# First stage of a two-block transformer kernel: positions loaded later, and the first chunk's second half fetched, rounded and split ahead of the second tokens' x

## The reference

```python
def rms_norm(x, g):
    xf = x.astype(jnp.float32)
    y = xf * lax.rsqrt(jnp.mean(xf * xf, axis=-1, keepdims=True) + NORM_EPS)
    return (y * g.astype(jnp.float32)).astype(x.dtype)

def moba_attention(xn, w_qkv, w_o, cos, sin):
    qkv = (xn @ w_qkv).reshape(b, s, 3, N_HEADS, HEAD_DIM)
    q, k, v = [jnp.transpose(qkv[:, :, i], (0, 2, 1, 3)) for i in range(3)]
    q = apply_partial_rope(q, cos, sin)
    k = apply_partial_rope(k, cos, sin)
    ...

def first_block(x, positions, norm_mix, ...):
    cos, sin = rope_tables(positions)
    for i in range(DEPTH):
        xn = rms_norm(x, norm_mix[i])
        ...
```

## Time and profile before

| what | value |
|---|---|
| device time, three runs | 1088.93, 1090.29 and 1090.34 us, median 1090.29 |
| profiled execution: first to last instruction (span) | 1086.7 us |
| PE busy | 1073.5 us, 99% of the span, 5810 matmuls |
| DVE busy | 740.5 us, 68% |
| ACT busy | 560.8 us, 52% |
| POOL busy | 40.2 us, 4% |
| data moved | 195.83 MB, 180 GB/s over the span |

### The profile page before, as it was taken

How to read it: one execution, slowest core, us unless ns; L and a number is a source line. 1 busy time by engine, 2 the same in 40 slices (tenths; PEclk the granted TensorE clock), 3 DMA queues, 4 the chain that set the end, 5 groups by cost and what they waited for, 6 DMA issues and landing times.

```text
span 1086.7 us, 15287 instructions
## 1 busy us (share of the span) xinstructions
PE 1073.5 (99%) x5810; PEld 908.4 (84%) x5810; DVE 740.5 (68%) x1044; ACT 560.8 (52%) x723; POOL 40.2 (4%) x59
## 2 busy tenths in 40 slices
PE   8999999999999999999999999999999999999997
PEld 6888888888888888888878888888889778888886
DVE  5756665656686656568877975665897878666665
ACT  5556444435455444346665544445653766444453
POOL 1000000000000000000000220000300300000000
PEclk9999999999999999999999999999999999999999
DMA  9953366564547564637532755657576324754651
GB/s 332 338 168 116 92 218 212 155 217 169 171 148 236 179 207 158 228 106 204 176 110 78 237 191 195 193 165 255 156 237 228 92 79 156 232 185 163 206 180 39
DMA packets 127162, 195.83 MB, mean 180 GB/s; under 512 B 6977, under 2 KB 97217, under 8 KB 126994
## 3 DMA queue, kind: packets, MB, share of 16 engines
q1 hardware_dynamic: 123904, 185.77, 51.8%
q0 software_dynamic: 3216, 9.51, 3.0%
q10 hardware_dynamic: 2, 0.00, 0.0%
HBM read 194.21 MB, written 1.05 MB: 180 GB/s over the span
## 4 chain that ended last, share of the span: by engine, by line
PE 95%; DVE 3%; ACT 1%; issue 1%; DVEq 0%; DMA 0%; ACTq 0%
PE ps L2099 25%; PE ps L2000 15%; PE ps L2002 15%; PE ps L2001 15%; PE ps L2102 13%; PE ps L2181 2%; PE ps L2220 1%; PE ps L2042 1%; PE ps L2597 1%; PE ps L2183 1%; DVE act L1237 1%; PE ps L2246 1%; PE ps L2595 1%; PE ps L2632 1%; PE ps L2279 1%
## 5 line engine op out<-in xcount | busy, mean ns | idle before, releaser
L2099 PE MATMUL ps<-act,whi 128*128 128x512 f32 x1200 | 424.4, 397 | 0.0
L1112 DVE TENSOR_TENSOR wlo<-raw,whi 128x2048 fp32r<-128x2048 f32 (+2 forms) x161 | 363.9, 2277 | 87.5 <-ACT whi L672 87.1
L2102 PE MATMUL ps<-act,wlo 128*128 128x256 f32 x1200 | 336.7, 281 | 0.0
L672 ACT ACTIVATE whi<-raw 128x2048 fp32r<-128x2048 f32 (+2 forms) x170 | 317.6, 1887 | 26.7 <-PE ps L2002 20.6
L2099 PEld LDWEIGHTS ps<-act,whi 128*128 128x128 f32 x1200 | 225.2, 188 | 53.7
L2102 PEld LDWEIGHTS ps<-act,wlo 128*128 128x128 f32 x1200 | 226.7, 189 | 2.0
L2002 PE MATMUL ps<-whi,hlo 128*128 128x512 f32 x400 | 157.1, 393 | 0.0
L2000 PE MATMUL ps<-whi,hhi 128*128 128x512 f32 x400 | 156.7, 392 | 0.1
L2001 PE MATMUL ps<-wlo,hhi 128*128 128x512 f32 x400 | 156.6, 392 | 0.0
L2000 PE MATMUL ps<-whi,act 128*128 128x512 f32 (+2 forms) x286 | 112.4, 393 | 1.5 <-DVE act L1812 0.6
L2002 PE MATMUL ps<-whi,act 128*128 128x512 f32 (+2 forms) x286 | 108.0, 378 | 0.0
(11 more groups left out here) (230 smaller groups left out, 1154.5 us busy)
## 6 DMA issues: line engine op xcount, KB each, us to landing
raw<-mlp_w_up_in SPq DMA_DIRECT2D x32, 1024.0 KB, 6.5
raw<-mlp_w_down_in SPq DMA_DIRECT2D x32, 1024.0 KB, 4.9
raw<-ffn_w_gate_in SPq DMA_DIRECT2D x22, 1024.0 KB, 5.4
raw<-ffn_w_up_in SPq DMA_DIRECT2D x22, 1024.0 KB, 5.3
raw<-ffn_w_down_in SPq DMA_DIRECT2D x22, 1024.0 KB, 4.9
raw<-attn_w_qkv_in SPq DMA_DIRECT2D x10, 1024.0 KB, 9.2
raw<-w_kv_shared_in SPq DMA_DIRECT2D x8, 1024.0 KB, 5.3
raw<-attn_w_o_in SPq DMA_DIRECT2D x4, 1024.0 KB, 5.0
```

The costliest lines, as they stand in the source:

```text
L672: nc.scalar.activation(whi[:, s, 0:width], raw[:, s, 0:width], ACT.Copy).then_inc(hi_ready, 1)
L1112: nc.vector.tensor_tensor(wlo[:, s, 0:width], raw[:, s, 0:width], whi[:, s, 0:width].bitcast(F32), ALU.subtract).then_inc(lo_ready, 1)
L2099: nc.tensor.matmul(bank(b + f), lhsT=w[0][:, at:at + P], rhs=act[:, k, :, :].rearrange("p a t -> p (a t)"), start=k == 0, stop=False, skip ...
L2102: ins = nc.tensor.matmul(bank(b + f, 0, T), lhsT=w[1][:, at:at + P], rhs=act_hi[:, k, :], start=False, stop=k == KT - 1, skip_group_check= ...
```

## The change

SP loads half b of chunk 0 ahead of the second tile's x. POOL issues the positions behind its wait for `hi_ready`. ACT rounds half b right after half a, ahead of its copies of quarters 1 and 2. DVE makes both low parts of chunk 0 right after the split of quarter 0, and then, for the second tile, x of quarter 2, split of 2, x of 3 and split of 1. PE signals each half of the spread gain row by itself; it runs two fillers ahead of quarter 0, six behind quarter 1 and none ahead of quarter 2; and it goes through chunks 0 and 1 tile by tile (all four row blocks of a chunk for one tile, then for the other), with quarter 2 transposed behind the first tile's products of chunk 0 and quarter 3 behind the second tile's first six.

```diff
@@ SP @@
             sp.dma_start(x[:, 0, :], x_rows[:, 0, :]).then_inc(x_loaded, 16)
             load_half(0, 0, first_half_loaded)
+            load_half(0, 1, w_loaded[SLOT[0]])
             sp.dma_start(x[:, 1, :], x_rows[:, 1, :]).then_inc(x_rest_loaded, 16)
-            load_half(0, 1, w_loaded[SLOT[0]])
             load_half(1, 0, second_half_loaded)
@@ POOL @@
+            pool.wait_ge(hi_ready, 2)
             for n, name in enumerate(("positions", "positions_2")):
                 pool.dma_start(pos_i[:, n, :], a[name].rearrange("a (t p) -> p (a t)", p=P),
                                allow_slow_non_contiguous=True).then_inc(pos_loaded, 16)
-            pool.wait_ge(hi_ready, 2)
@@ ACT @@
             copy_turned("mix0", (0,))
             hi_part_of(0, 0, first_half_loaded, first_half_hi)
-            copy_turned("mix0", (1, 2))
             hi_part_of(0, 1, w_loaded[SLOT[0]], hi_ready)
+            copy_turned("mix0", (1,))
+            copy_turned("mix0", (2,))
             hi_part_of(1, 0, second_half_loaded, second_half_hi)
             copy_turned("mix0", (3,))
@@ DVE @@
             first_gained(0)
+            dve.wait_ge(first_row_spread, 2)
             first_gained(1)
             split_turned("mix0", (0,))
+            lo_part_of(0, 0, first_half_hi, 1, first_half_lo)
+            lo_part_of(0, 1, hi_ready, 1, lo_ready)
             dve.wait_ge(x_rest_loaded, 16)
             dve.sem_inc(x_ready, 2)
             first_gained(2)
-            lo_part_of(0, 0, first_half_hi, 1, first_half_lo)
+            split_turned("mix0", (2,))
+            first_gained(3)
             split_turned("mix0", (1,))
-            first_gained(3)
-            split_turned("mix0", (2,))
-            lo_part_of(0, 1, hi_ready, 1, lo_ready)
             dve.wait_ge(xs_ready, 4 * XSR["mix0"] + 4)
@@ PE, turn @@
                     for h in range(2):
-                        ins = nc.tensor.matmul(bank(2 + h), lhsT=scale_row[0:1, 0:P],
-                                               rhs=rows[0:1, 0, h * HALF:(h + 1) * HALF], start=True, stop=True)
-                    ins.then_inc(first_row_spread, 1)
+                        nc.tensor.matmul(bank(2 + h), lhsT=scale_row[0:1, 0:P],
+                                         rhs=rows[0:1, 0, h * HALF:(h + 1) * HALF], start=True, stop=True)\
+                            .then_inc(first_row_spread, 1)
                     pe.wait_ge(const_loaded, 16)
@@
                     if name == "mix0":
-                        for _ in range((3, 0, 3, 0)[p]):
+                        for _ in range((2, 0, 0, 0)[p]):
                             nc.tensor.matmul(bank(7, 0, P), lhsT=ident, rhs=ident, start=True, stop=True)
@@ PE, first stage @@
-            turn("mix0", parts=(0, 1, 2))
+            turn("mix0", parts=(0, 1))
+            for _ in range(6):
+                nc.tensor.matmul(bank(7, 0, P), lhsT=ident, rhs=ident, start=True, stop=True)
@@ PE, qkv_products @@
-                    for h in range(2):
-                        pe.wait_ge(*((lo_ready, c + 1) if h else (half_lo, 1)))
-                        for t in range(TT):
-                            if h == 0:
-                                wait_acts("mix0", c + 1 + 2 * t)
+                    for t in range(TT):
+                        wait_acts("mix0", c + 1 + 2 * t)
+                        for h in range(2):
+                            pe.wait_ge(*((lo_ready, c + 1) if h else (half_lo, 1)))
                             for k in range(2 * h, 2 * h + 2):
                                 ...
-                            if c == 0 and h == 0 and t == 1:
-                                turn("mix0", parts=(3,))
+                            if c == 0 and h != t:
+                                turn("mix0", parts=(2 + t,))
```

## The result

The changed kernel takes 1094.14 us (median of five runs, 1093.64 to 1094.95), the kernel before 1090.0 in the same session (five runs, 1088.93 to 1090.34): a ratio of 1.0041, 95% interval 1.003 to 1.0052. The change makes the kernel slower by 4.1 us; 1093.7 was forecast. The profiled execution, the fastest of the five, took 1093.64 with a span of 1091.7.

What follows compares the result with a forecast made beforehand. TensorE, holding 95% of the chain of waits, was taken to bound the kernel. 2.6 us later at chunk 2 plus 0.8 at chunk 4 gave 3.4, from 1090.29 to 1093.7 us; range 1091.2 to 1096.8.

Steps and rivals of the forecast that it cites:

- The first product: TensorE's first product in the first stage comes at 10.90 instead of 11.59, 0.69 us earlier.
- The gap: TensorE stands 2.84 us behind quarter 2's transposes, through four uncovered hand-offs, until the second tile's product at 16.98.
- Chunk 1's second half: On TensorE, a further wait of 0.4 for quarter 3's copy, rounding and low part; product at 21.98.
- Chunk 2: Its products start on TensorE at 26.08 where the old order had 23.46, 2.6 later.
- Chunk 4: Its products wait for VectorE's copy of chunk 0 and 1's result until 37.81; TensorE arrives at 37.02: 0.8 more.
- The sum of 3.4: Whole first stage: 2.6 later at chunk 2 plus 0.8 at chunk 4, 3.4 us slower.
- The positions: Issued by GpSimd at 21.0 and 21.8, transfer 7.1, landed at 28.9 before the cast at 29.4: no cost.
- The rival of 10 us: Rival, chance 0.18: positions take 10.0 to land, the cast waits to 31.8, 2.4 more: 1096.1.
- I count that at nothing, as the path above does not wait for a DMA: At the start, moving the positions' packets away can only make half b land earlier; counted as no gain.
- the clock's fall as a rival with 0.10: Rival, chance 0.10: TensorE's clock falls in the new wait, 1.7 more, 1095.4; twice as long, 1097.1.
- the prediction's own sign: Forecast is wrong if products behind TensorE's new wait step by twice 0.228.
- Fillers behind quarter 1: Six fillers on TensorE end between 10.0 and 11.2, taken as 10.3; the upper end would give back 0.3.

Runs made afterwards that it cites:

- the first: Changed kernel with quarter 2 transposed between the first tile's two groups of six products, not behind both: 1091.8 us, 1.0023 of the kernel before.
- the second: Changed kernel with VectorE's split of quarter 1 moved ahead of the second tile's x: 1091.71 us, 1.0023 of the kernel before.
- both together: Changed kernel with quarter 2 transposed between the first tile's sixes and quarter 1 split ahead of the second tile's x: 1091.27 us, 1.0019 of the kernel before.
- The rebuilt order: Changed kernel with half a rounded and split earlier, quarter 2 between the sixes, VectorE reordered, two fillers behind quarter 1: 1088.8 us, 0.9994 of the kernel before.
- the gap filled: Changed kernel with ten f32 filler matmuls on TensorE behind quarter 2, while it waits for the second tile: 1093.33 us, 1.0038 of the kernel before.

## Why the prediction was right, and where it was not

- **The first product,** forecast at 10.90: 11.02. DVE's low part began at 9.65 (9.63), and the product followed 1.37 later where the step was taken as 1.27.
- **The gap,** the main term: a product at 16.98 after 2.84 us; measured 17.05, and 13.84 + 0.35 to 17.05 are 2.86. The edits that take links out of it show that it is this chain: the first takes 1.2 off the ruler, the second 1.2 off the wait, both together 1.7 off the ruler.
- **Chunk 1's second half:** 21.98 forecast, 22.02 measured. **Chunk 2:** 26.08 forecast, 26.23 measured. **Chunk 4:** 37.81 forecast, 37.89 measured. The sum of 3.4 was 3.5 at that row and 3.65 at the ruler, in the profile with the clock up. (The lower edge of the forecast, 1092.6, is 1092.5 by its own terms, 1090.29 + 2.2.)
- **The positions:** no cost, as taken; the landing was 5.8 us, not 7.1. The rival of 10 us is out: the cast lists no wait. By the Trainium skill ("DMA: Bandwidth & Descriptors", section on queues, rings and completion order) the small transfer should not stand behind the weight stream, and it did not: it landed within 5.8 us, while the row load issued right behind it, at 22.60, took 11.5. The stream was thin then, 27 GB/s from 21 to 24 us, so this is a mild test. The rebuilt order is a harder one: there the positions went out from 15.78 on into a full stream (385 to 388 GB/s from 14 to 19 us, 339 to 363 from 19 to 22) and landed after 5.2 and 5.5 us.
- **"I count that at nothing, as the path above does not wait for a DMA".** True of the old order, where the late positions alone change nothing. For the new order the argument was incomplete: it looked at the landing of half b, and not at that of half a, which the new order wants at 8.57 instead of 8.98, only 0.5 us after its old landing at 8.07. In the one profile with early positions half a did come late and the first product with it; the times show no such cost, so whether the term is nothing in most executions stays open. The forecast did not depend on it, because the change moves the positions too.
- **The weakest step: the clock's fall as a rival with 0.10 and not a term of the sum.** By the prediction's own sign, products behind the gap that step by twice 0.228, the forecast was wrong in two of three profiles of the changed kernel (0.43). The rival's mechanism is right and its price near (1.7 forecast; 1.5 in the products behind the gap, 1.5 between the medians with the gap filled and open). The row that spoke against it, a gap of 1.64 at full clock, was no bound for 2.61. The Trainium skill ("TensorE: Matmul & The Clock Gate", section on oscillation in real kernels) warns that a wait between groups of products throttles the next group: the 0.51 and 0.52 behind the gap in the second and third profile agree with it, the 1.00 of the first does not.
- **Fillers behind quarter 1** were counted as cover that might cost 0.3. They ended at 8.69 + 1.62 = 10.31, as taken (10.3), and cost nothing here. Without them the clock fell in the profile's first tile too: the ruler is 2.9 later than in the first profile of the changed kernel and 1.0 later than in the other two. In the two executions without them at 1092.7, where the mean granted clock was 0.999, they were not missed.

With the clock up the change costs 3.65 by the ruler, with it down 5.1 when the late gain row is taken off. The medians of its three timings stand 4.1, 4.8 and 5.7 above the kernel before, the last beyond this band by 0.6; the forecast of 3.4 lies just below it. The terms of the first stage were right by their mechanism. That the total was close as well was in part luck: the term that the sum lacked happened to be small, and the range was wide enough for it. What decides in which execution the clock falls stays open, and so does why the tail behind the ruler takes 775.2 us in one profile and 777.2 in another: the granted clock from 304 us on is 1.00 in the first profiles of both kernels, where the tail took 775.9 and 777.2.

## What to carry to other kernels

Count the engine hand-offs between a transposed block's production and its first use, and place the transposes so early that other products cover that chain; a whole tile's products ahead of the transposes are no cover if the next tile's chain starts only when they end. A gap costs its length and can cost the clock behind it (here never at 1.64 us or less, mostly at 2.61), so price both, and where it cannot be closed, filler matmuls inside it can save the second part. A load's slack is a property of the order: when a consumer moves up, work out again by how much each of its loads lands ahead of the need.

## What the runs showed of the hardware that was not expected

- The same idle time of 2.61 us on TensorE left the upper level in one profile of the changed kernel (granted 1.00 behind it) and the lower one in two others (0.51 and 0.52), and in those with early positions (0.55 from 18.87 to 22.00) and without the six fillers (0.50 from 19.70 to 22.70). In the first of the changed kernel's profiles the twelve fillers ahead had taken 1.62 us, in the other two 2.16 and 2.11; with 1.22 and 1.41 us idle the level held although the fillers took 2.40 and 2.77. What decides was not separated.
- The lower level can set in late: 1.47 us after the engine resumed (12.60 - 11.13) in the kernel without fillers.
- In the old order, two transfers of 1 KB each, in single integers, went with a stream of 94 and 103 GB/s from 4.80 to 6.60 us in two profiles, at 0.90 and 0.82 busy engines; without them one profile had 289 at 1.00. Half a (512 KB) landed after 6.4, 6.1 and, without them, 4.7 us. As the new order shows landings of 5.9 and 6.6 without them too, this is a likely effect, from few profiles.
